# One 512-column matmul for an operand's high and low part in four more projections, and gate logarithms taken straight from the sigmoid

## Chip, cores and metric

The kernel runs on one core of a Trainium2 chip. The metric is the device time of one execution in microseconds (us), the median of the runs shown. The engines are named as the profile names them: PE (TensorE, matmuls), DVE (VectorE), ACT (ScalarE), POOL (GpSimd) and SP (SyncE, which issues DMAs). Each runs its own instructions in order and waits on semaphores for the others.

## The reference, cut to what matters

Two blocks of a network work on one sequence of 256 tokens with 2048 channels, all in float32. The first block:

```python
mod = silu(c) @ w_ada + b_ada                      # sh1, sc1, g1, sh2, sc2, g2
z = (x * (1 + sc1) + sh1) @ w_in + b_in            # 2048 -> 9216: u, v, z_h, z_g
y_a = (gelu(u) * spatial_mix(layer_norm(gelu(v)))) @ w_branch_a
y_b = hyena(short_conv(z_h)) @ w_branch_b          # long convolutions by FFT
mix = (sigmoid(g_a) * y_a + sigmoid(g_b) * y_b) @ w_o + b_o
x = layer_norm(ALPHA * x + g1 * mix)
f = square(relu((x * (1 + sc2) + sh2) @ w_m1 + b_m1)) @ w_m2 + b_m2
x = layer_norm(ALPHA * x + g2 * f)
```

The second block has two layers. The first is a gated convolution: `h @ conv_w_in` (2048 to 6144), a depthwise convolution of 31 taps, a norm, a gate, `@ conv_w_out`. The second is a linear attention with 16 heads of 128 channels, in two directions:

```python
q, a_f, a_b, i, z = split(rms_norm(x) @ hgrn_w_in)           # 2048 -> 10240
log_f = logaddexp(log(lb), log1p(-lb) + log_sigmoid(a))      # = log(lb + (1 - lb) * sigmoid(a))
key = (1 - lb) * sigmoid(-a)
# with b = cumsum(log_f): scores[t, s] = sum over channels of q_t * key_s * exp(b_t - b_s)
o = rms_norm(o_fwd + o_bwd) * o_norm
x = x + (o * silu(z)) @ hgrn_w_out
```

## The kernel before

Activations lie with channels on the 128 partitions and the 256 tokens along a row. To keep float32 accuracy with PE's faster fp32r format, every operand is split into a high part (rounded to fp32r) and a low part (the rest). A product is the sum of three: high weights times high operand, high weights times low operand, low weights times high operand.

Weights stream once through the kernel, in "halves": a half is 8 tiles of 128x128 (512 KB) and holds one half of the input channels of one output block of 128 channels. SP loads halves in the order of the list `HALVES` into a ring of 4, later 6 slots; for each, ACT writes the high part `wh` (L1640, `hi(h)`) and DVE the low part `wl` (L942, `lo(h)`), four buffers each, three halves ahead of PE. An output block of a projection of 2048 channels is two halves, 16 tiles k. Between the halves, in the first block up to the middle of `w_o` and in the first half of the MLP, SP also loads "chunks" of `w_ada`, 512 KB each, and DVE adds one a block (L961, `add_chunk`).

PE accumulates an output block in one of three PSUM banks (`ps[0]` to `ps[2]`). The list `MAIN` says which semaphore tells that a bank is free, and PE's `bank()` waits for the use three before. A bank has 512 columns, and a block 256.

Two forms of the inner loop exist. `half` does three matmuls of 256 columns for each k (L528, L529, L530) into 256 columns of the bank. `wide_half`, in the MLP alone, sends the operand's high and low part through PE as one matmul of 512 columns (L541), and the low weights with the high part as one of 256 (L543) into the first half of the bank. Whoever empties a wide bank adds its two halves: in the MLP ACT reads columns 256:512 (with bias or scale) and DVE adds columns 0:256 (L1338, L1357).

In the input projection (`N_IN`, 72 blocks, the first 24 of them for the hyena branch) ACT empties the bank in one instruction: Identity with the bias for blocks 0 to 23 (L1757), after which DVE does the short convolution (L1084, L1086, L1088), Gelu for 24 to 39 (L1759), Sigmoid for 40 to 71 (L1761). The FFT work of `hyena()` and the spatial gating of `spatial()` are woven in between the blocks as generators. Squares for the variance of the spatial gating are taken by ACT (L1722) and summed by PE (L581).

In the heads (`HG_PARTS`, 5 parts of 2 halves for each of 16 heads, 10 halves a head) the order of the head's own work is written out by `HEAD_PLAN`: head hd makes its step s behind half 10*hd + 6 + s ("tick"), on every engine, for 22 steps. So a head begins at tick 6 of its ten, while two older ones are still under way. Its steps on each engine:

- After part 4 (tick 5) DVE scales the gates (L1577, L1581), ACT takes two sigmoids and a third for z (L2059, L2061, L2065). DVE then computes lb + (1 - lb) * sigmoid (L1591) and its maximum with 2^-64 (L1593), and the keys (L1598).
- Step 0: ACT takes Ln of both gates (L2006). Step 1: DVE sums them up (L1534).
- Steps 1 to 14, nine levels: DVE differences (L1517), ACT exponentials (L2022), POOL products (L2231, L2233), PE scores (L879) into one of three banks, and DVE's predicated copy (L1527) that empties it. PE's next score into a bank waits for the copy of the level three before.
- Steps 16 to 21: PE multiplies with the values (L888), ACT squares (L2027), PE sums (L581), ACT takes Sqrt (L2035), DVE the reciprocal (L1545) and two products (L1548, L1552), ACT and POOL split the result (L2040, L2083).

ACT works with function tables; an ACT_TABLE_LOAD row stands ahead of a function whose table isn't loaded. In the last projection three output blocks (`NEARLY`) start early, between the last head's steps, and ask for all three banks at once.

Of the kernel before, what the change touches and what calls it, by code (L numbers as in the profile page):

```python
# [18 lines left out]
ALPHA = 2.0 ** 0.25  # L19
# [128 lines left out]
HEAD_STEPS = 22  # L148
# [17 lines left out]
def n_rest(k):  # L166
# [21 lines left out]
    "hmade_v hmade_a zin zh uv gate "  # L188
# [3 lines left out]
    "ablo gy mx woe gp "  # L192

    "lg rel rad rsq m2e res "
# [3 lines left out]
    "lbd lbt hg sm sp szs f2 f3 kk0 kk1 zz qq vi "  # L198
    "ln0 ln1 cum0 cum1 dif0 dif1 exp0 exp1 kq0 kq1 sco0 sco1 pla0 pla1 plv0 plv1 vtr vcp "
    "om osq ocp oss osd orc on"  # L200
# [35 lines left out]
def _build(nc, ctx, d, out):  # L236
# [76 lines left out]
    gate = lambda i: BF[:, 40 + i, :] if i < 24 else XR[:, i - 16, :]  # L313
    pad = [misc[:, 2048 + 260 * i:2048 + 260 * i + 258] for i in range(2)]
# [29 lines left out]
    lbtab = misc[:, 512:640]  # L344
    one_row = misc[:, 768:1024]
# [46 lines left out]
    for n in range(16):  # L392
        MAIN.append((s.woe, n + 1))
        if n == 8:
            MAIN.append((s.mod, 10))
# [25 lines left out]
    def wait_placed(w, hd, li):  # L421
        u = hd % 2
        if li == 0:
            w.wait_ge((s.pla0, s.pla1)[u], hd // 2 + 1)
        else:
            w.wait_ge((s.plv0, s.plv1)[u], 8 * (hd // 2) + li)

# [84 lines left out]
    def tensor_program(e):  # L512
# [20 lines left out]


        def wide_half(h, pb, both, ready, first, last):
            hi, lo = wh[h % NSPLIT], wl[h % NSPLIT]
            w.wait_ge(s.lo, h + 1)
            for k in range(8):
                ready(k)
                xs = both(k)  # L540
                e.matmul(pb.rearrange("p (a t) -> p a t", a=2), hi[:, k, :], xs, start=first and k == 0,  # L541
                         stop=False)
                done = e.matmul(pb[:, 0:256], lo[:, k, :], xs[:, 0, :], start=False, stop=last and k == 7)  # L543
            done.then_inc(s.mm, 1)


        def two_halves(h, first, second, ready, begin, end, behind=lambda k: None):
            for j in range(2):
                w.wait_ge(s.lo, h + j + 1)
            for k in range(8):  # L550
                ready(k)
                for j, (pb, xs) in enumerate(((first, A2), (second, A2))):
                    hi, lo = wh[(h + j) % NSPLIT], wl[(h + j) % NSPLIT]
                    x = xs[:, :, 8 * (not begin) + k, :]
                    if pb.shape[1] == 512:
                        e.matmul(pb.rearrange("p (a t) -> p a t", a=2), hi[:, k, :], x, start=begin and k == 0, stop=False)
                    else:
                        e.matmul(pb, hi[:, k, :], x[:, 0, :], start=begin and k == 0, stop=False)
                        e.matmul(pb, hi[:, k, :], x[:, 1, :], start=False, stop=False)
                    done = e.matmul(pb[:, 0:256], lo[:, k, :], x[:, 0, :], start=False, stop=end and k == 7)  # L560
# [13 lines left out]
        def a_tiles(part):  # L574
            return lambda k: (Ah[:, 8 * part + k, :], Al[:, 8 * part + k, :])

        def b_tiles(base):
            return lambda k: (Bh[:, base + k, :], Bl[:, base + k, :])
# [117 lines left out]
        for i, n in enumerate(N_IN):  # L696
            pb = bank()[:, 0:256]
            for part in range(2):
                half(2 * i + part, pb, a_tiles(part), lambda k: wait_lo(w, 8 * part + k, 0),
                     part == 0, part == 1)  # L700
                if part == 0:
                    if 33 <= i < 41:
                        w.wait_ge(s.uv, i - 24)
                        w.wait_ge(s.spec, 16)
                        row_sum(ps[3][:, 0:256], 1, vv(i - 33), i - 33, 8, s.vmean)
# [53 lines left out]
        for n in range(16):  # L759
            pb = bank()[:, 0:256]  # L760
# [12 lines left out]
        for fh in range(2):  # L773
# [4 lines left out]
            for n in range(2, 32):  # L778
                pb = bank()[:]
                for part in range(2):  # L780
                    wide_half(H_M1[fh] + 2 * n + part, pb, lambda k: A2[:, :, 8 * part + k, :],
# [1542 lines left out]
```

## Time and profile before

| | |
|---|---|
| median of 3 runs | 2782.59 us (2781.21 to 2788.07) |
| the profiled execution | 2780.93 us, its span 2779.1 us |
| mean granted TensorE clock | 0.967 |
| PE busy | 2582.7 us, 93% of the span |
| weight loads on PE busy | 2430.1 us, 87% |
| DVE busy | 2018.7 us, 73% |
| ACT busy | 1401.7 us, 50% |
| POOL busy | 840.3 us, 30% |
| DMA | 534.84 MB, mean 192 GB/s |

A row of the timeline has the start, the duration, the engine, the line, the operation, what it writes and reads, how many such instructions follow each other, and in brackets how long the engine was idle before and what ended the wait. Two matmuls overlap, so the distance of their starts, not their duration, tells the pace. Stages by time: filters and `w_ada` to 137, input projection to 655, the two branches' projection to 757, `w_o` to 856, MLP to 1613, convolution input to 1966, convolution output to 2096, heads to 2657, last projection to the end.

### The profile page before, as it was taken

The page shows a single profiled execution, that of the slowest core. Times are in us where ns is not written, and L with a number is a line of the kernel's source. Part 1 is how long each engine was busy: PE and PEld are TensorE (multiplying, and loading weights), DVE is VectorE, ACT ScalarE, POOL GpSimd, SP SyncE. Part 2 cuts the span into 40 slices and gives each one's busy share as a digit, 9 for nine tenths or more (in the row PEclk, how much of TensorE's full clock was granted, in tenths as well). Part 3 has the DMA queues.
Part 4 walks back from the last instruction along what each step waited for, and adds up shares of the span by engine and source line. Part 5 has one row for each costly group of instructions (what it writes and reads, how often), then busy time and mean ns, then how long its engine had stood idle before and what let it go on. Part 6 is the DMA issues. An engine that isn't in the chain of part 4 may idle for free.

```text
span 2779.1 us, 46348 instructions
## 1 busy us (share of the span) xinstructions
PE 2582.7 (93%) x18408; PEld 2430.1 (87%) x18408; DVE 2018.7 (73%) x2576; ACT 1401.7 (50%) x2108; POOL 840.3 (30%) x780
## 2 busy tenths in 40 slices
PE   4599998999997999999999979997799999999989
PEld 1489998999996888888888879987699999999979
DVE  7888765767867876555555568887657899999964
ACT  0154323344435543444544456666556777777753
POOL 0100000001214621001101058888102666666630
PEclk9799999999998999999999989999899999999989
DMA  9978754787873877665566535554355444444434
GB/s 320 340 257 268 231 200 156 239 267 242 270 246 116 291 258 227 190 189 183 190 194 189 185 101 167 167 159 128 102 171 158 150 152 152 150 147 149 148 105 146
DMA packets 146353, 534.84 MB, mean 192 GB/s; under 512 B 16631, under 2 KB 16792, under 8 KB 145688
## 3 DMA queue, kind: packets, MB, share of 16 engines
q1 hardware_dynamic: 143176, 520.33, 58.2%
q0 software_dynamic: 2960, 11.54, 1.2%
q8 instruction: 146, 2.39, 0.3%
q14 instruction: 71, 0.58, 0.1%
HBM read 525.51 MB, written 6.29 MB: 191 GB/s over the span
## 4 chain that ended last, share of the span: by engine, by line
PE 58%; DVE 16%; issue 7%; POOL 7%; ACT 6%; DMA 5%; SPq 0%; POOLq 0%; DVEq 0%; ACTq 0%
PE ps L541 13%; PE ps L528 11%; PE ps L530 10%; PE ps L529 10%; PE ps L543 7%; DVE wl L942 5%; POOL misc L2200 5%; DMA ring<-in_w_ada 4%; ACT wh L1640 2%; DVE AF L961 1%; PE ps L581 1%; DVE BF L1527 1%; PE ps L663 1%; PE ps L651 1%; DVE BF L1517 1%
## 5 line engine op out<-in xcount | busy, mean ns | idle before, releaser
L942 DVE TENSOR_TENSOR wl<-ring,wh 128x1024 fp32r<-128x1024 f32 x784 | 1031.4, 1328 | 381.7 <-ACT wh L1640 380.8
L528 PE MATMUL ps<-A,wh 128*128 128x256 f32 x3424 | 997.2, 291 | 17.0 <-DVE wl L942 10.4
L1640 ACT CAST wh<-ring 128x1024 fp32r<-128x1024 f32 x784 | 814.8, 1043 | 381.5 <-PE ps L530 212.2
L529 PE MATMUL ps<-A,wh 128*128 128x256 f32 x3424 | 974.4, 285 | 0.0
L530 PE MATMUL ps<-A,wl 128*128 128x256 f32 x3424 | 974.3, 285 | 0.0
L528 PEld LDWEIGHTS ps<-A,wh 128*128 128x128 f32 x3424 | 663.1, 194 | 21.8 <-issue 10.8
L529 PEld LDWEIGHTS ps<-A,wh 128*128 128x128 f32 x3424 | 663.3, 194 | 1.2
L530 PEld LDWEIGHTS ps<-A,wl 128*128 128x128 f32 x3424 | 662.2, 193 | 0.0
L541 PE MATMUL ps<-B,wh 128*128 128x512 f32 x1024 | 357.9, 394 | 0.0
L541 PE MATMUL ps<-A,wh 128*128 128x512 f32 x960 | 337.5, 396 | 2.2 <-DVE wl L942 2.2
L543 PE MATMUL ps<-B,wl 128*128 128x256 f32 x1024 | 287.3, 281 | 0.0
L543 PE MATMUL ps<-A,wl 128*128 128x256 f32 x960 | 269.5, 281 | 0.0
L528 PE MATMUL ps<-B,wh 128*128 128x256 f32 x768 | 228.9, 298 | 21.3 <-DVE B L946 7.3
L2200 POOL TENSOR_TENSOR misc<-misc 128x256 f32<-128x256 f32 x224 | 226.7, 1012 | 55.8 <-ACT misc L1915 28.3
L2083 POOL TENSOR_TENSOR B<-tmpA,B 128x256 fp32r<-128x256 f32 x80 | 80.2, 1002 | 524.7 <-ACT B L1867 447.5
L541 PEld LDWEIGHTS ps<-B,wh 128*128 128x128 f32 x1024 | 192.9, 188 | 42.8
L529 PE MATMUL ps<-B,wh 128*128 128x256 f32 x768 | 222.6, 290 | 0.0
L530 PE MATMUL ps<-B,wl 128*128 128x256 f32 x768 | 222.5, 290 | 0.0
L541 PEld LDWEIGHTS ps<-A,wh 128*128 128x128 f32 x960 | 181.2, 189 | 44.6 <-DVE wl L942 2.8
L543 PEld LDWEIGHTS ps<-B,wl 128*128 128x128 f32 x1024 | 194.6, 190 | 0.0
L2231 POOL TENSOR_TENSOR BF<-BF 128x256 f32<-128x256 f32 x128 | 152.5, 1191 | 137.9 <-ACT BF L2022 104.8
L543 PEld LDWEIGHTS ps<-A,wl 128*128 128x128 f32 x960 | 182.4, 190 | 0.0
(247 smaller groups left out, 3323.3 us busy)
## 6 DMA issues: line engine op xcount, KB each, us to landing
ring<-in_w_m SPq DMA_DIRECT2D x256, 512.0 KB, 4.5
ring<-in_hgrn_w_in SPq DMA_DIRECT2D x160, 512.0 KB, 3.8
ring<-in_w_ada SPq DMA_DIRECT2D x144, 512.0 KB, 6.6
ring<-in_w_in SPq DMA_DIRECT2D x144, 512.0 KB, 4.9
ring<-in_conv_w_in SPq DMA_DIRECT2D x96, 512.0 KB, 3.9
AF<-in_w_ada SPq DMA_DIRECT2D x48, 512.0 KB, 9.1
ring<-in_w_ab SPq DMA_DIRECT2D x32, 512.0 KB, 5.2
ring<-in_w_o SPq DMA_DIRECT2D x32, 512.0 KB, 5.4
```

The lines of the kernel that those rows point to most:

```text
L528: e.matmul(dst, hi[:, k, :], xh, start=first and k == 0, stop=False)
L529: e.matmul(dst, hi[:, k, :], xl, start=False, stop=False)
L530: done = e.matmul(dst, lo[:, k, :], xh, start=False, stop=last and k == 7)
L541: e.matmul(pb.rearrange("p (a t) -> p a t", a=2), hi[:, k, :], xs, start=first and k == 0, stop=False)
L543: done = e.matmul(pb[:, 0:256], lo[:, k, :], xs[:, 0, :], start=False, stop=last and k == 7)
L581: e.matmul(bank_ap, ones[:, row, :], tile, start=i == 0, stop=i == n - 1).then_inc(signal, 1)
L651: done = e.matmul(ps[5 + ri][:, mm * 256:mm * 256 + 256], dft[:, 2 * ri + tt, mm * P:mm * P + P], ut[:, tt, :], start=tt == 0, stop=tt == 1)
L942: e.tensor_tensor(low[:], ring[SLOT[h]][:], hi[:].bitcast(F32), ALU.subtract).then_inc(s.lo, 1)
L1640: e.copy(wh[h % NSPLIT][:], ring[SLOT[h]][:]).then_inc(s.hi, 1)
L2083: e.tensor_tensor(low, src, hi.bitcast(F32), ALU.subtract).then_inc(signal, 1)
L2200: padd.up(e.tensor_tensor(pa, pa, ptmp[padd.n % NTMP], ALU.add))
L2231: e.tensor_tensor(sides(BF, at(u, 10 + x), h, h), sides(BF, at(u, 1), h, 256 + h), sides(BF, ev, h, 256 + h), ALU.mult).then_inc(kq, 1)
```

## The change

Four more projections use the wide form: the input projection, `w_o`, the convolution's output and the last one. `half` and `wide_half` become one, with the choice by the width of the target:

```diff
+        def k_tile(dst, hi, lo, x, first, last):
+            if dst.shape[1] == 512:
+                e.matmul(dst.rearrange("p (a t) -> p a t", a=2), hi, x, start=first, stop=False)
+            else:
+                e.matmul(dst, hi, x[:, 0, :], start=first, stop=False)
+                e.matmul(dst, hi, x[:, 1, :], start=False, stop=False)
+            return e.matmul(dst[:, 0:256], lo, x[:, 0, :], start=False, stop=last)
...
-                xh, xl = tiles(k)
-                e.matmul(dst, hi[:, k, :], xh, start=first and k == 0, stop=False)
-                e.matmul(dst, hi[:, k, :], xl, start=False, stop=False)
-                done = e.matmul(dst, lo[:, k, :], xh, start=False, stop=last and k == 7)
+                done = k_tile(dst, hi[:, k, :], lo[:, k, :], tiles(k), first and k == 0, last and k == 7)
```

Input projection: ACT writes columns 256:512 plus the bias, DVE adds columns 0:256, and Gelu or Sigmoid is applied one block later, in place. A bank is now free after DVE's addition (`MAIN`), and the mean of v is summed by PE one block later.

```diff
-        MAIN.append((s.zin, i + 1) if i < 24 else (s.uv, i - 23) if i < 40 else (s.gate, i - 39))
+        MAIN.append((s.zin, i + 1) if i < 24 else (s.pre, i - 23))
...
+        def add_halves(i, dst, pb):
+            w.wait_ge(s.ev, i + 1)
+            return e.tensor_tensor(dst, dst, pb[:, 0:256], ALU.add)
...
             if i < 24:
+                add_halves(i, pad[i % 2][:, 1:257], pb).then_inc(s.zin, 1)
                 short_conv(i, pad[i % 2], zh(i))
+            else:
+                add_halves(i, in_tile(n), pb).then_inc(s.pre, 1)
...
+        def nonlinear(i):
+            x = in_tile(N_IN[i])
+            w.wait_ge(s.pre, i - 23)
+            if i < 40:
+                e.activation(x, x, ACT.Gelu).then_inc(s.uv, 1)
+            else:
+                e.activation(x, x, ACT.Sigmoid).then_inc(s.gate, 1)
...
-                e.activation(pad[i % 2][:, 1:257], pb, ACT.Identity, bias=col("b_in", n)).then_inc(s.zin, 1)
-            elif i < 40:
-                e.activation(uu(n) if n < 8 else vv(n - 8), pb, ACT.Gelu, bias=col("b_in", n)).then_inc(s.uv, 1)
+                e.activation(pad[i % 2][:, 1:257], pb, ACT.Identity, bias=col("b_in", n)).then_inc(s.ev, 1)
             else:
-                e.activation(gate(n - ZG), pb, ACT.Sigmoid, bias=col("b_in", n)).then_inc(s.gate, 1)
+                e.activation(in_tile(n), pb, ACT.Identity, bias=col("b_in", n)).then_inc(s.ev, 1)
+            if i >= 25:
+                nonlinear(i - 1)
```

`w_o` (and the second MLP projection, where it stood already) on DVE, and the two residual projections:

```diff
+        def both_halves(n, alpha, evicted, pb, factor):
+            w.wait_ge(s.ev, evicted)
+            own.up(e.scalar_tensor_tensor(XR[:, n, :], XR[:, n, :], alpha, tmpA[n % 4][:], ALU.mult, ALU.add))
+            w.wait_ge(s.own, own.n)
+            e.scalar_tensor_tensor(XR[:, n, :], pb[:, 0:256], factor, XR[:, n, :], ALU.mult, ALU.add).then_inc(s.xr, 1)
...
+        def add_out(n, pb):
+            own.up(e.tensor_tensor(XR[:, n, :], XR[:, n, :], pb[:, 256:512], ALU.add))
+            w.wait_ge(s.own, own.n)
+            e.tensor_tensor(XR[:, n, :], XR[:, n, :], pb[:, 0:256], ALU.add).then_inc(s.xr, 1)
```

Heads: DVE's L1591 and L1593 go; ACT's Ln reads the sigmoid with (1 - lb) as its scale and lb as its bias, and lb is raised to at least 2^-64 once in the table. The deviation becomes Ln and Exp of -0.5 on ACT, and DVE's reciprocal goes. All of this comes one step later (24 steps instead of 22), and ACT takes the heads of a tick in another order: a head at step 0 first, then one beyond step 15, then the rest.

```diff
-                    w.wait_ge(s.sp, hd + 1)
+                    w.wait_ge(s.sm, hd + 1)
                     w.wait_ge(s.lbt, 4)
...
-                        own.up(e.tensor_scalar(x, x, om, lb, ALU.mult, ALU.add))
-                        w.wait_ge(s.own, own.n)
-                        e.tensor_scalar(slot(u, 6 + k), x, 2.0 ** -64, None, ALU.max).then_inc((s.f2, s.f3)[u], 1)
...
+            for k in range(2):
+                e.activation(slot(u, 6 + k), sig[0][:, 256 * k:256 * k + 256], ACT.Ln,
+                             scale=lbtab[:, 32 * k + 16 + hd:32 * k + 17 + hd],
+                             bias=lbtab[:, 32 * k + hd:32 * k + hd + 1]).then_inc((s.ln0, s.ln1)[u], 1)
...
-            e.activation(ost[u], mean_ap, ACT.Sqrt, scale=1.0 / 128, bias=sm[:, 1:2]).then_inc(s.osd, 1)
+            e.activation(ost[u], mean_ap, ACT.Ln, scale=1.0 / 128, bias=sm[:, 1:2]).then_inc(s.ols, 1)
+            w.wait_ge(s.ols, hd + 1)
+            e.activation(ost[u], ost[u], ACT.Exp, scale=-0.5).then_inc(s.osd, 1)
...
-            e.reciprocal(ost[u], ost[u]).then_inc(s.orc, 1)
-            w.wait_ge(s.orc, hd + 1)
...
-            for hd, _ in HEAD_PLAN[tick]:
+            for hd, step in sorted(HEAD_PLAN[tick], key=lambda x: 0 if x[1] == 0 else 1 if x[1] > 15 else 2):
```

The branches' projection, the convolution's input and the heads' input keep three matmuls of 256 columns.

## Rows read from the trace of the kernel before

**Rows 1.** Windows: PE, PEld, DVE, ACT, POOL busy (x); clock, DMA share, GB/s.

```profile
165.70:240.50 74.80, 74.80 (x626) 74.80 (x625) 64.50 (x80) 32.03 (x39) 0.00 (x0) 1.00 0.84 278
...
2189.20:2651.90 462.70, 448.67 (x3745) 445.69 (x3744) 431.50 (x533) 337.30 (x533) 281.11 (x247) 1.00 0.49 149
```

**Rows 2.** What ended PE's idle time before L879 (us, times).

```profile
  DVE BF L1527: 15.1, 14
```

**Rows 3.** Timeline of ACT, input projection, first and last of 14 evictions.

```profile
165.68 0.48 ACT L1757 ACTIVATE misc<-ps,vec 128x256 f32<-128x256 f32 x1 [1.78 <-PE ps L530]
...
240.56 0.48 ACT L1757 ACTIVATE misc<-ps,vec 128x256 f32<-128x256 f32 x1 [1.77 <-PE ps L530]
```

**Rows 4.** Timeline of DVE, MLP projection without chunks, first and last of nine.

```profile
1302.33 0.42 DVE L1338 TENSOR_TENSOR tmpA<-ps,tmpA 128x256 f32<-128x256 f32 x1 [0.88 <-ACT tmpA L1865]
...
1346.71 0.42 DVE L1338 TENSOR_TENSOR tmpA<-ps,tmpA 128x256 f32<-128x256 f32 x1 [0.88 <-ACT tmpA L1865]
```

**Rows 5.** Timeline of DVE, one block of the input projection.

```profile
206.51 0.41 DVE L1084 TENSOR_SCALAR BF<-misc,vec 128x256 f32<-128x256 f32 x1 [0.84 <-ACT misc L1757]
...
208.17 1.28 DVE L961 SCALAR_TENSOR_TENSOR XR<-ring,cnd,XR 128x1024 f32<-128x1024 f32 x1 [0.20 <-DMA ring<-in_w_ada]
...
209.37 2.35 DVE L942 TENSOR_TENSOR wl<-ring,wh 128x1024 fp32r<-128x1024 f32 x2
```

**Rows 6.** DMA issues in 930:1070: count, KB, median us to landing.

```profile
ring<-in_w_ada SPq DMA_DIRECT2D x24, 512.0 KB, 6.8
```

**Rows 7.** Timeline of DVE, MLP projection with chunks, first and last of eleven.

```profile
919.37 0.41 DVE L1338 TENSOR_TENSOR tmpA<-ps,tmpA 128x256 f32<-128x256 f32 x1
...
974.31 0.42 DVE L1338 TENSOR_TENSOR tmpA<-ps,tmpA 128x256 f32<-128x256 f32 x1 [0.28 <-ACT tmpA L1865]
```

**Rows 8.** Timeline of ACT, around the first gate blocks.

```profile
427.59 1.28 ACT L1761 ACT_TABLE_LOAD   x1
...
447.34 0.47 ACT L1761 ACTIVATE BF<-ps,vec 128x256 f32<-128x256 f32 x1 [4.27 <-PE ps L530]
```

**Rows 9.** Timeline of PE, the second sum of squares.

```profile
451.60 2.39 PE L581 MATMUL ps<-misc,ones 128*128 128x256 f32 x8 [0.99 <-ACT misc L1722]
```

**Rows 10.** Timeline of DVE, `w_o`, the first residual.

```profile
771.30 0.43 DVE L1225 SCALAR_TENSOR_TENSOR XR<-XR,tmpA 128x256 f32<-128x256 f32 x1 [9.11 <-DMA XR<-in_x]
```

**Rows 11.** Timeline of PE, behind `w_o`.

```profile
864.64 1.22 PE L751 MATMUL ps<-misc,ones 128*128 128x256 f32 x2 [8.17 <-POOL misc L2139]
```

**Rows 12.** Timeline of PE, heads: before and at the wait, behind part 4.

```profile
2224.58 0.28 PE L528 MATMUL ps<-A,wh 128*128 128x256 f32 x1
...
2226.18 0.68 PE L879 MATMUL ps<-BF 128*128 128x128 f32 x4 [1.08 <-DVE BF L1527]
...
2250.58 0.50 PE L879 MATMUL ps<-BF 128*128 128x128 f32 x3
```

**Rows 13.** Timeline of DVE, the same head and the next.

```profile
2222.95 1.75 DVE L1545 RECIPROCAL misc<-misc 128x256 f32<-128x256 f32 x1
...
2225.59 0.43 DVE L1527 COPY_PREDICATED BF<-masks,ps 128x256 f32<-128x256 uint8 x1
...
2254.66 0.41 DVE L1591 TENSOR_SCALAR misc<-misc 128x256 f32<-128x256 f32 x1 [2.21 <-ACT misc L2061]
...
2256.89 0.61 DVE L1598 TENSOR_SCALAR BF<-misc 128x256 f32<-128x256 f32 x2
```

**Rows 14.** Timeline of ACT, table loads of a head.

```profile
2248.16 1.28 ACT L2035 ACT_TABLE_LOAD   x1
...
2252.03 1.28 ACT L2059 ACT_TABLE_LOAD   x1
...
2255.89 1.28 ACT L2006 ACT_TABLE_LOAD   x1
```

**Rows 15.** Timeline of PE, behind the last head's last half.

```profile
2662.82 0.55 PE L528 MATMUL ps<-B,wh 128*128 128x256 f32 x1 [5.36 <-issue]
```

**Rows 16.** Timeline of DVE, the last head's values.

```profile
2662.20 0.41 DVE L1606 TENSOR_TENSOR misc<-ps,statb 128x256 f32<-128x256 f32 x1
```

More of the change, by code:

```diff
@@ L553, in two_halves @@
                     hi, lo = wh[(h + j) % NSPLIT], wl[(h + j) % NSPLIT]
[L554 to L560, printed above, removed]
+                    done = k_tile(pb, hi[:, k, :], lo[:, k, :], xs[:, :, 8 * (not begin) + k, :], begin and k == 0,
+                                  end and k == 7)
                     if k == 7:
@@ L780, in tensor_program @@
                 for part in range(2):
-                    wide_half(H_M1[fh] + 2 * n + part, pb, lambda k: A2[:, :, 8 * part + k, :],
+                    half(H_M1[fh] + 2 * n + part, pb, a_tiles(part),
                               lambda k: wait_lo(w, 8 * part + k, 1), part == 0, part == 1)
@@ L838, in next_square @@
             row_sum(mean_ap, 2, lsq[0][:, n % 2 * T:n % 2 * T + T], n, 16, s.sqs)
+        conv_tile = lambda k: Bl.rearrange("p (a k) t -> p a k t", a=2)[:, :, k, :]
         for n in range(16):
-            pb = bank()[:, 0:256]
+            pb = bank()[:]
             for part in range(2):
-                half(H_CO + 2 * n + part, pb, lambda k: (Bl[:, 8 * part + k, :], Bl[:, 16 + 8 * part + k, :]),
+                half(H_CO + 2 * n + part, pb, lambda k: conv_tile(8 * part + k),
                      lambda k: wait_lo(w, 8 * part + k, 3), part == 0, part == 1)
@@ L915, in tensor_program @@
                     heads_behind(x)
-        early = [bank()[:, 0:256] for n in range(NEARLY)]
+        early = [bank()[:] for n in range(NEARLY)]
         done_heads = lambda k: w.wait_ge(s.blo, 85 + k + 1)
@@ L1288, in vector_program @@
             w.wait_ge(s.khat, 144)
-            residual(n, ALPHA if n < 12 else 1.0, s.woe, n + 1)
+            both_halves(n, ALPHA if n < 12 else 1.0, EV_O + n + 1, pb, mod[:, 32 + n:33 + n])
             if n < 8:
@@ L1541, in head @@
                 yield
-            for _ in range(4):
+            for _ in range(5):
                 yield
             w.wait_ge(s.osd, hd + 1)
-            e.reciprocal(ost[u], ost[u]).then_inc(s.orc, 1)
-            w.wait_ge(s.orc, hd + 1)
             w.wait_ge(s.ocp, hd + 1)
@@ L1825, in scalar_program @@
             e.activation(tmpA[n % 4][:], pb, ACT.Identity, scale=mod[:, 32 + n:33 + n],
[L1826 removed]
+                         bias=gb[:, n:n + 1]).then_inc(s.ev, 1)
             squares_early(n, 0)
@@ L1864, in scalar_program @@
                 w.wait_ge(s.blo, 21 + 32 * fh + n - 3)
-                e.activation(tmpA[n % 4][:], pb, ACT.Identity, bias=col("b_m1", 32 * fh + n)).then_inc(s.rel, 1)
+                e.activation(tmpA[n % 4][:], pb, ACT.Identity, bias=col("b_m1", 32 * fh + n)).then_inc(s.ev, 1)
                 w.wait_ge(s.rsq, 32 * fh + n + 1)
@@ L1876, in scalar_program @@
                 if fh:
-                    e.activation(tmpA[n % 4][:], pb, ACT.Identity, scale=mod[:, 80 + n:81 + n]).then_inc(s.m2e, 1)
+                    e.activation(tmpA[n % 4][:], pb, ACT.Identity, scale=mod[:, 80 + n:81 + n]).then_inc(s.ev, 1)
                     squares_early(n, 1)
@@ L2235, in head @@
                 yield
-            for _ in range(5):
+            for _ in range(6):
                 yield
```

96 lines of the change are left out of this document (39 added, 57 removed).

## Prediction

> **What bounds the kernel now.** I read the page's first part (the table above), then the windows, then the timelines of single engines stage by stage. TensorE (PE) fills 100% of the input projection (165.7:240.5) and 97% of the heads (2189.2:2651.9), where DVE is at 93%, both at a granted clock of 1.00, the 2.4 GHz level [rows 1]. So two things can be won: PE time itself, and the few waits in which PE stands still. The biggest repeated one is L879 (a head's scores) behind L1527 (a predicated copy on DVE): 15.1 us in 14 times [rows 2].
>
> **Term 1, the matmuls.** In the projections that change, one weight tile k costs three matmuls of 256 columns; afterwards one of 512 and one of 256. Before, ACT's evictions L1757 go from 165.68 to 240.56 in 13 periods: 5.760 us for the 16 tiles of one output block [rows 3]. The wide form already runs in the MLP: DVE's L1338 goes from 1302.33 to 1346.71 in 8 periods, 5.547 us for 16 tiles [rows 4]. The difference is 0.213 us a block (13.3 ns a tile). I take it whole wherever PE sets the pace.
>
> Here the Trainium skill speaks against the size. "TensorE: Matmul & The Clock Gate", Back-to-back issue gap, puts the warm gap of isolated matmuls at N/2.4 + 2.5 ns, so one matmul less would give 2.5 ns a tile and not 13.3; for 1920 tiles 4.8 us against 25.6. The rows of this kernel show 13.3 with the same operands, each matmul with its weight load, and I go by them.
>
> *Input projection, 72 blocks.* Block 0 waits for its operand, so it gains nothing: 71 x 0.213 = 15.1. What the halves' addition adds: one DVE operation a block. Its price is that of L1338, which also adds a PSUM half, 0.42, with the wait between dependent operations 0.45. DVE's round from L1084 at 206.51 to the end of the pair at 211.72 is 5.21, of it 0.20 a wait for a DMA [rows 5]: 5.01 + 0.45 = 5.46, under 5.547, with 0.09 to spare. The chunk of w_ada is the next thing that can be late: its median to landing is 6.8 us in the MLP's first half, which loads the same two halves and one chunk a block [rows 6], and there L1338 goes from 919.37 to 974.31 in 10 periods, 5.49 [rows 7]. So the DMA queue has carried this pace. I charge 0.7 us for 24 blocks; the ends are 0 and 5.1 (no gain in them at all). From block 24 on ACT writes Identity, DVE adds, and ACT applies Gelu or Sigmoid a block later: 0.47 more a block on an ACT that is 43% busy [rows 1, 8] and hidden by the three halves of weights that lie ready. One spot isn't: the first Sigmoid's table load, 1.28, stands at 427.59 in ACT's idle time now. Afterwards it comes behind the eviction of block 41 (447.34), ahead of the weight cast that DVE and then the squares wait for; PE waits for these squares at 451.60 [rows 8, 9]. Charge: 1.28 + 0.47, rounded to 1.7; ends 0 and 1.8. Sum of the stage: 15.1 - 0.7 - 1.7 = 12.7.
>
> *w_o, 16 blocks.* DVE stands until x has landed by DMA at 771.3 [rows 10], PE runs dry behind it, and the weight low part it needs lies behind L1225 in DVE's queue. Blocks 0 and 1 gain nothing (the landing doesn't move), and the second operation of `both_halves` (0.45, as above) makes the restart later. At the end PE waits 8.17 us for POOL's chain of sums L2139 [rows 11], which starts with the squares of block 14, so block 15 gains nothing. 13 x 0.213 - 0.45 = 2.3.
>
> *Convolution output, 16 blocks.* Block 0 waits for its operand. The second addition lies inside each block's slack, but not behind the last: 15 x 0.213 - 0.45 = 2.7.
>
> *Last projection, 16 blocks.* 13 ordinary ones, 2.8; of the three early ones (0.6), which run between the steps of the last head, I take 0.3; the last addition ahead of the output costs 0.45: 2.6.
>
> Term 1 together: 12.7 + 2.3 + 2.7 + 2.6 = 20.3 us.
>
> **Term 2, the heads.** At 2224.58 PE starts a weight tile; the next group would start 0.36 later and starts at 2226.18, 1.24 late, and takes 0.07 longer: 1.31 us [rows 12]. DVE is what is late: it spends 1.75 on the reciprocal L1545 and 0.9 on two products, and L1527 ends at 2226.02. Ahead of that it waits 2.21 for the second sigmoid and does L1591 and L1593 twice, 2.2 us (2254.66 to 2256.89 in the next head) [rows 13]. The change takes both away: the gate's affine part goes into ACT's scale and bias, the floor 2^-64 into the table, the reciprocal into Ln and Exp of -0.5. DVE drops 1.75 + 2.2 = 3.95 us of 33 a head (431.5 over 13 heads).
>
> ACT's order changes too. Now a head has five table loads of 1.28, four of them for Sqrt, Exp, Sigmoid and Ln between 2248.16 and 2257.17 [rows 14]. The sorting puts the gates' Ln, then the deviation's Ln and Exp of an older head, in one tick: Sigmoid, Ln, Exp, three loads. That saves 2.56 and adds about 0.47 (Exp) and 0.3 (two Ln for one).
>
> The Trainium skill, "ScalarE: Activation LUTs", Table sets: the hidden batching unit, says that one set holds both ln and exp. This kernel's rows show a load between its Ln and its Exp all the same, so I count three loads; by the page it would be two, and the margin below 1.28 wider.
>
> What is late next: counted from PE's L879 behind part 4 (2250.58, [rows 12]), with durations as they stand, L1577 ends by about 1.6, the three sigmoids by 3.3, ACT's weight cast by 4.3; DVE's low part 5.5 and the copy that stalled PE 5.9, needed at 9.9, three halves of 3.3 on. ACT goes on: Ln's load 5.6, three Ln 6.9, Exp's load 8.2, Exp 8.65, the next cast 9.65; then DVE's low part 10.85, the head's two products 11.75, the next copy 12.1. PE needs that copy at 13.3 and those weights at 13.7. So the wait goes, with 1.2 us to spare. POOL (281 of 463 us busy) isn't near. Of the 14 waits 13 are worth 1.31. Behind the last head PE stands 5.36 us until 2662.82 because all three banks are asked for and the third is free only after L1606, which ends at 2662.61 [rows 15, 16]; that DVE work comes only 0.3 earlier while PE comes 1.3 earlier. 13 x 1.31 + 0.3 = 17.3. Ends: 5 (the margin is missed by a microsecond in each head) and 22 (the wait for the banks halves as well). The tail of the last head trades a Sqrt and the reciprocal (1.75) for Ln, a load (1.28) and Exp: nothing.
>
> **Sum.** 20.3 + 17.3 = 37.6. The profiled execution took 2780.93 (span 2779.1 and 1.8 around it), so 2743.3. The median of the runs shown is 1.7 above it: 2745.
>
> **Rivals.** (a) The chain of ACT in the heads is longer than 8.65, and part of the wait stays: DVE now waits for Exp where it computed the reciprocal itself. For it: 1.2 us of margin in a chain of twelve steps; against it: ACT has lost two loads. Up to 12 us less: 2748 to 2757. (b) DVE and the chunks bind in the input projection: 0.09 us of spare on DVE is thin. Up to 5 us less: 2750. (c) The wait for the banks behind the last head, and the low clock after it, shrink with DVE's load: 3 to 6 us more, 2739 to 2742. (d) The wide pair is no cheaper in the changed stages than three matmuls: the 112 blocks lose 0.213 each, 2745 + 24 = 2769; only another behaviour of PE than in [rows 4] could do it. The Trainium skill's gap (above) would leave 2.5 of the 13.3 ns: by it 2765. (e) The other side: ACT's burst between Sigmoid and the next weight cast becomes PE's wait. PE has 3 us until the weights of that tick (10.85 against 13.7); to reach the time before, the burst must eat these 2.9, the 1.31, and 20.3 / 14 = 1.45 more, so it decides from 5.7 us beyond my chain, over four table loads a head more than I count. That would be 2783 and above.
>
> **How the numbers follow.** Forecast 0.55, (a) 0.20, (b) 0.09, (c) 0.08, (d) 0.03, (e) 0.05. The forecast's own range is 2741 to 2750. The range that leaves out 2 in 10 at most is 2737 to 2760: (c) below, (a) above. A measurement of this kernel tells about 0.3%, 8.3 us, from no change. Faster by more than that means under 2774: 0.91; within it 0.05 ((a) and (d) together, part of (e)); slower 0.04.
>
> **What would show it.** A profile after should have blocks of 5.55 us in evictions of the input projection and in the last projection, a period of a head of 34.3 for now 35.6, no idle time of L879 behind L1527, three table loads a head, DVE at some 85% in the heads, and a longer wait at 451.60. I am wrong if the head's period stays above 35, if L528's place shows waits for weight low parts L942 in the first 24 blocks, or if ACT loads a table between the gates' Ln and the deviation's Ln.

## The result: 15 us faster where 38 were forecast

| | before | after |
|---|---|---|
| median, both in the same set of runs | 2786.95 us (5 runs) | 2772.03 us (2767.39 to 2772.26, 5 runs) |
| once more, in another set (below) | 2786.39 us (11 runs) | 2769.71 us (2763.65 to 2776.41, 6 runs) |
| profiled execution | 2780.93 us | 2772.07 us, span 2770.3 us |
| PE busy | 2582.7 us | 2567.9 us |
| DVE busy | 2018.7 us | 2016.2 us |
| ACT busy | 1401.7 us | 1393.4 us |

The ratio is 0.9947, 95% interval 0.9934 to 0.996, so 14.9 us; the second set gives 0.9944 (0.9922 to 0.9965), 16.7 us. The forecast, 2745 us and 2737 to 2760, is missed by 27 us: 22.7 are missing gain (14.9 where 37.6 were forecast), and 4.4 come from where it started, a median before of 2782.59 us from three runs where five give 2786.95. The two profiled executions differ by 8.9 us only, and they differ in more than the change (the pace of wide tiles and the late chunks, below). So the profiles show mechanisms, and the medians what the change is worth.

The windows that answer to [rows 1]: input projection, and the heads up to 2640.

```profile
165.70:240.50 74.80, 74.25 (x429) 64.63 (x427) 71.89 (x98) 33.39 (x41) 0.00 (x0) 1.00 0.85 286
2189.20:2640.00 450.80, 441.34 (x3688) 438.36 (x3687) 388.13 (x466) 305.36 (x524) 272.54 (x245) 1.00 0.46 151
```

PE still stands still in the heads (441 of 451 us), while DVE's share has fallen from 93% to 86%.

ACT's evictions in the input projection, first and last of 14, which answer to [rows 3]:

```profile
165.11 0.48 ACT L1759 ACTIVATE misc<-ps,vec 128x256 f32<-128x256 f32 x1 [1.67 <-PE ps L535]
...
237.22 0.48 ACT L1759 ACTIVATE misc<-ps,vec 128x256 f32<-128x256 f32 x1 [1.66 <-PE ps L535]
```

13 periods of 5.547 us, the same as those of [rows 4]: the wide pair does give 0.213 us a block in the new place too. The same unchanged loop of the MLP that gave 5.547 before is slower now, DVE's first and last of nine:

```profile
1299.80 0.42 DVE L1344 TENSOR_TENSOR tmpA<-ps,tmpA 128x256 f32<-128x256 f32 x1 [0.97 <-ACT tmpA L1868]
...
1345.03 0.42 DVE L1344 TENSOR_TENSOR tmpA<-ps,tmpA 128x256 f32<-128x256 f32 x1 [0.98 <-ACT tmpA L1868]
```

45.23 / 8 = 5.654 us, at a granted clock of 1.00. Between 1260 and 1550 us this costs 5 us.

In the heads, waits from 2220 to 2560 us (total, times, longest), which answer to [rows 2]:

```profile
DVE wl L938 <- ACT wh L1634: 46.1, 19, 3.5
...
PE ps L858 <- ACT misc L2040: 7.8, 10, 0.8
...
DVE BF L1595 <- ACT misc L2073: 3.3, 9, 0.4
```

The wait of the scores for DVE's copy is gone, as forecast. In its place PE waits for ACT's copy of the older head's output (L2040) before it transposes the values (L858):

```profile
2241.69 0.41 PE L858 MATMUL ps<-ident,misc 128*128 128x128 f32 x2 [0.79 <-ACT misc L2040]
```

The row to look at is the first of the three, though: DVE now waits 46 us for ACT's weight casts. DVE's timeline shows a head's period (its sums L1540) and the two waits in it; ACT's shows what stands ahead of the second cast, which answers to [rows 14], and where ACT itself waits for DVE.

```profile
2225.74 1.76 DVE L1540 TENSOR_TENSOR_SCAN misc<-misc,BF 128x256 f32<-128x256 f32 x2
...
2253.22 1.62 DVE L938 TENSOR_TENSOR wl<-ring,wh 128x1024 fp32r<-128x1024 f32 x1 [1.29 <-ACT wh L1634]
...
2258.65 1.22 DVE L938 TENSOR_TENSOR wl<-ring,wh 128x1024 fp32r<-128x1024 f32 x1 [3.44 <-ACT wh L1634]
...
2260.98 1.77 DVE L1540 TENSOR_TENSOR_SCAN misc<-misc,BF 128x256 f32<-128x256 f32 x2
```

```profile
2250.65 0.63 ACT L2073 ACTIVATE misc<-misc 128x512 f32<-128x512 f32 x1 [0.67 <-DVE misc L1584]
...
2252.15 1.03 ACT L1634 CAST wh<-ring 128x1024 fp32r<-128x1024 f32 x1
2253.20 1.28 ACT L2014 ACT_TABLE_LOAD   x1
2254.50 1.09 ACT L2014 ACTIVATE BF<-misc 128x256 f32<-128x256 f32 x2
2255.50 0.45 ACT L2046 ACTIVATE misc<-ps,sm 128x256 f32<-128x256 f32 x1
2255.97 1.28 ACT L2048 ACT_TABLE_LOAD   x1
2257.26 0.42 ACT L2048 ACTIVATE misc<-misc 128x256 f32<-128x256 f32 x1
2257.59 1.98 ACT L1634 CAST wh<-ring 128x1024 fp32r<-128x1024 f32 x2
```

A head takes 35.27 us (mean of ten), for 35.61 before and 34.3 forecast. DVE idles 5.1 us in it: 0.37, 1.29 and 3.44. So its own work is 30.2. Before, DVE idled 2.2 us a head, all in one place ([rows 13]), and its own work was 33.4. In both kernels the period is DVE's own work plus DVE's waits for ACT: 33.4 + 2.2 = 35.6 and 30.2 + 5.1 = 35.3. Such a sum alone proves nothing, since work and idle time make up the period on every engine. What it adds is whom DVE waits for: never for PE or POOL, only for instructions of ACT, and ACT's chain in front of them starts with a wait for DVE's L1584. So the two can form a closed round that keeps its length whatever PE does. Call this **DVE's round** (theory A). The competing reading (theory B) is the forecast's: PE has a period of its own, 34.3, and loses what it waits at one spot.

For the projections the profile shows late chunks. PE's sums over w_ada, one in the input projection, one in `w_o`, one in the MLP:

```profile
241.14 1.58 PE L566 MATMUL ps<-ones,XR 128*128 128x1 f32 x13 [1.18 <-DVE XR L957]
...
802.59 2.07 PE L566 MATMUL ps<-ones,misc 128*128 128x1 f32 x14 [0.79 <-DVE misc L957]
...
973.37 1.84 PE L566 MATMUL ps<-ones,misc 128*128 128x1 f32 x8 [4.75 <-DVE misc L957]
```

Behind the first two, windows of the same kernel (before, both stretches were at 1.00):

```profile
244.00:246.00 2.00, 2.00 (x8) 1.72 (x7) 0.40 (x1) 0.00 (x0) 0.00 (x0) 0.50 0.67 236
...
805.00:810.00 5.00, 5.00 (x17) 4.23 (x17) 1.31 (x2) 0.00 (x0) 0.00 (x0) 0.50 0.62 202
```

The clock stands at 0.50, the 1.2 GHz level. The wide tiles' starts, counted against 0.347 us a tile, give its cost: 1.6 us at 244, 2.7 at 805 and 2.2 at 977 (the expectation of experiment 6 puts the three at 1.5, 2.3 and 1.7).

### The profile page after: what moved, and what is told of

Its sections match the earlier page's. It is cut to its first block, busy times and chain, and to the rows that moved or that the text cites. A ratio compares the mean times of both kernels' runs of the same rounds, so it can differ in the third digit from the quotient of the medians.

```text
span 2770.3 us, 42622 instructions
## 1 busy us (share of the span) xinstructions
PE 2567.9 (93%) x16488; PEld 2321.7 (84%) x16488; DVE 2016.2 (73%) x2617; ACT 1393.4 (50%) x2161; POOL 814.7 (29%) x780
## 4 chain that ended last, share of the span: by engine, by line
PE 64%; DVE 12%; POOL 7%; issue 6%; ACT 6%; DMA 5%; SPq 0%; POOLq 0%; DVEq 0%; ACTq 0%
PE ps L531 29%; PE ps L535 19%; POOL misc L2214 5%; PE ps L533 4%; PE ps L534 4%; DVE wl L938 4%; DMA ring<-in_w_ada 3%; ACT wh L1634 2%; PE ps L576 2%; DVE AF L957 2%; PE ps L875 1%; PE ps L658 1%; PE ps L566 1%; POOL misc L2153 1%; PE ps L646 1%
## 5 line engine op out<-in xcount | busy, mean ns | idle before, releaser
L938 DVE TENSOR_TENSOR wl<-ring,wh 128x1024 fp32r<-128x1024 f32 x784 | 1036.7, 1335 | 398.9 <-ACT wh L1634 357.6
L531 PE MATMUL ps<-A,wh 128*128 128x512 f32 x2176 | 780.7, 403 | 19.1 <-DVE A L942 9.0
L533 PE MATMUL ps<-A,wh 128*128 128x256 f32 x2304 | 677.3, 294 | 15.7 <-DVE A L942 10.6
L531 PE MATMUL ps<-B,wh 128*128 128x512 f32 x1792 | 645.6, 404 | 22.9 <-DVE B L942 7.3
L534 PE MATMUL ps<-A,wh 128*128 128x256 f32 x2304 | 657.2, 285 | 0.0
L531 PEld LDWEIGHTS ps<-A,wh 128*128 128x128 f32 x2176 | 414.2, 190 | 121.0 <-issue 14.4
L533 PEld LDWEIGHTS ps<-A,wh 128*128 128x128 f32 x2304 | 447.6, 194 | 20.6 <-issue 11.6
L534 PEld LDWEIGHTS ps<-A,wh 128*128 128x128 f32 x2304 | 447.7, 194 | 1.2
L531 PEld LDWEIGHTS ps<-B,wh 128*128 128x128 f32 x1792 | 342.6, 191 | 108.0 <-issue 11.7
L535 PEld LDWEIGHTS ps<-B,wl 128*128 128x128 f32 x1792 | 345.4, 193 | 0.5
L2214 POOL TENSOR_TENSOR misc<-misc 128x256 f32<-128x256 f32 x224 | 226.7, 1012 | 55.8 <-ACT misc L1918 28.2
L2245 POOL TENSOR_TENSOR BF<-BF 128x256 f32<-128x256 f32 x128 | 154.8, 1209 | 110.6 <-ACT BF L2032 68.4
L2247 POOL TENSOR_TENSOR BF<-BF 128x256 f32<-128x256 f32 x128 | 148.1, 1157 | 0.0
L1918 ACT ACTIVATE misc<-misc,vec 128x256 f32<-128x256 f32 x240 | 109.7, 501 | 54.9 <-POOL misc L2214 30.2
L1523 DVE TENSOR_TENSOR BF<-misc 128x512 f32<-128x512 f32 x128 | 121.3, 948 | 4.3 <-POOL BF L2247 3.8
L957 DVE SCALAR_TENSOR_TENSOR XR<-ring,cnd,XR 128x1024 f32<-128x1024 f32 x75 | 96.0, 1280 | 6.0 <-DMA ring<-in_w_ada 5.7
```

The lines of the kernel that those rows point to most:

```text
L531: e.matmul(dst.rearrange("p (a t) -> p a t", a=2), hi, x, start=first, stop=False)
L533: e.matmul(dst, hi, x[:, 0, :], start=first, stop=False)
L534: e.matmul(dst, hi, x[:, 1, :], start=False, stop=False)
L535: return e.matmul(dst[:, 0:256], lo, x[:, 0, :], start=False, stop=last)
L938: e.tensor_tensor(low[:], ring[SLOT[h]][:], hi[:].bitcast(F32), ALU.subtract).then_inc(s.lo, 1)
L957: chunks.up(e.scalar_tensor_tensor(acc, wt, cnd[:, k:k + 1], acc, ALU.mult, ALU.add))
```

## The experiments

All times are medians. The first four kernels ran together (before: 2788.27 us, 17 runs), the next four (before: 2786.39, 11 runs) and the last four (before: 2785.87, 19 runs) too.

**1 and 2. Each half of the change alone.** The first has all edits outside the heads, the second only those in the heads.

> The four projections take the wide form, the heads stay as they were. If the gains of the two parts simply add, this kernel is faster than the one before by what the marks of the two traces give the projections: 8.1 us in the input projection, 2.8 in the convolution's output, 2.7 in the last one, against 1.4 lost in w_o and 3.6 at the late chunk in the MLP; together 8 to 10 us. My forecast had 20.3 us. If the loss lies in something that the two parts do to each other, this kernel alone would show the 20 us.

> Only the heads change, the projections keep three matmuls of 256. Theory A (DVE's round sets the head's period: its own work and its waits for ACT, 33.4 + 2.2 us before, 30.2 + 5.1 after): period 35.3 for 35.6, 4 to 6 us faster in all. Theory B (my forecast: PE's own 34.3 us once the copies aren't late, and the missing rest is an effect of the wide projections around): 17 us faster.

Projections alone: 2773.73 us, ratio 0.9945 (0.9927 to 0.9963), 14.5 us faster, with 10 to 20 in the interval. Heads alone: 2782.25 us, 0.998 (0.9964 to 0.9995), 6.0 us faster, with 1.4 to 10. The head's period is 35.60 in the first and 35.28 in the second. So the heads gave about a third of their 17.3 us with nothing wide around them: theory A's number. The two medians add up to 20.5 us where the whole change has 14.9 and 16.7, which the three intervals allow. The projections gave more than the 8 to 10 us that I had read from one pair of profiles, and the forecast's 20.3 is at the edge of their interval.

**3. ACT's weight cast earlier.** `hi` is what casts a half. The last two lines of the diff are DVE's order in the tick.

```diff
-                    hi(H_HG + x + 3)
+                    if hd < 2 or x % 10 != 7:
+                        hi(H_HG + x + 3)
...
             e.activation(ost[u], mean_ap, ACT.Ln, scale=1.0 / 128, bias=sm[:, 1:2]).then_inc(s.ols, 1)
+            if hd < 14:
+                hi(H_HG + 10 * hd + 30)
             w.wait_ge(s.ols, hd + 1)
...
-            for hd, _ in HEAD_PLAN[tick]:
+            for hd, step in sorted(HEAD_PLAN[tick], key=lambda x: x[1] > 15):
```

> The kernel after, with ACT's weight cast of tick 7 pulled ahead of the second table load (between the two logarithms and the exponential of the deviation), and DVE taking the new head's sums ahead of the old head's two products in that tick. No work is removed. Theory A (DVE's round): DVE's 3.4 us wait for that cast shrinks to about 1.5, its round to some 33.4, so the head's period falls from 35.3 to PE's own 34.2 to 34.4 and the kernel gains 11 to 14 us on the one after. Theory B (PE's wait for the copy of the last head's output on ACT sets the period by itself): that copy's place on ACT isn't touched, so the period stays at 35.3 and the time too.

2757.59 us, ratio 0.9892 (0.9872 to 0.9912): 30.7 us under the kernel before, where the kernel after is 14.9 and 16.7 under it; so 14 to 16 us of gain, where theory A said 11 to 14. From the first to the last head's sums the trace is 15.2 us shorter than the one after. DVE's timeline has both waits shorter, and the next head 34.30 us on:

```profile
2228.59 1.27 DVE L1540 TENSOR_TENSOR_SCAN misc<-misc,BF 128x256 f32<-128x256 f32 x2
...
2257.71 1.23 DVE L938 TENSOR_TENSOR wl<-ring,wh 128x1024 fp32r<-128x1024 f32 x1 [0.72 <-ACT wh L1634]
...
2261.41 1.23 DVE L938 TENSOR_TENSOR wl<-ring,wh 128x1024 fp32r<-128x1024 f32 x1 [2.11 <-ACT wh L1634]
...
2262.89 1.26 DVE L1540 TENSOR_TENSOR_SCAN misc<-misc,BF 128x256 f32<-128x256 f32 x2
```

Its window of the heads:

```profile
2189.20:2640.00 450.80, 450.80 (x3789) 450.08 (x3788) 395.51 (x472) 319.31 (x540) 285.97 (x248) 1.00 0.47 154
```

PE is busy all the time, L2040's place on ACT was not touched, and PE's wait for it is gone. DVE now waits for PE too, 0.5 us in each head before L1584, which it never did in the kernel after. The period is the 34.3 of the forecast: now PE sets it.

**4. The transposition a step later.** PE's `step` first, then that of ACT's copy of the values.

```diff
-                if step == 6:
+                if step == 7:
...
-                if step == 7:
+                if step == 8:
```

> The kernel after, with PE's transposition of the values (and ACT's copy of them) one step later, so that the new wait of PE for ACT's copy of the older head's output is gone. Theory A (DVE's round): PE's wait goes elsewhere, behind a copy or a weight low part of DVE, the period stays 35.2 to 35.3 and the time within 2 us of the kernel after. Theory B (this wait sets the period): 34.2 to 34.4, 13 us faster than the one after.

2770.08 us, ratio 0.9935 (0.9916 to 0.9954): 18.2 us under the kernel before, so 1.5 to 3.3 us beyond the kernel after, which is within the noise. The wait for L2040 is gone and the period is unchanged, 35.26 us:

```profile
2255.17 1.76 DVE L1540 TENSOR_TENSOR_SCAN misc<-misc,BF 128x256 f32<-128x256 f32 x2
2290.44 1.76 DVE L1540 TENSOR_TENSOR_SCAN misc<-misc,BF 128x256 f32<-128x256 f32 x2
```

So the wait at which PE stood was not what cost the time. Removed, half of it comes back in other places (0.4 us of 0.8 in each head, behind L1533 and L938 of DVE), and DVE's three waits are what they were. Theory B falls.

**5. The kernel after once more.**

> The kernel after once more, unchanged, beside the kernels of this call. The pace of a wide weight tile (a matmul of 512 and one of 256) took one of two values in all profiles so far, 347 or 353 ns, for stretches of 30 to 300 us. If that is a matter of the execution, the profiled execution has its 353 ns stretches at other places than the first one had (1260 to 1540 us), and the execution's time moves by 6.6 ns for each tile in them; if it is a matter of the program, they are at the same places.

2769.71 us. The profile (2776.41 us) has the slow pace from 240 to 300, 880 to 980, 1260 to 1550 and 2700 us to the end; the first one had it from 760 to 800, 980 to 1070 and 1260 to 1550. Those are the longer stretches; one program, two patterns, with the longest stretch in common.

**6. The sums later.** PE's `reduce_chunks` and DVE's `bias` of blocks 16, 32, 48 and 64 of the input projection, of block 8 of `w_o` and block 16 of the MLP move from behind the block's first half to behind its second:

```diff
-                    if i in n_ada:
-                        reduce_chunks(n_ada[i])
...
+            if i in n_ada:
+                reduce_chunks(n_ada[i])
```

> The kernel after, with PE's sums over w_ada's chunks (and DVE's bias behind them) moved half an output block back in the input projection, w_o and the first MLP projection. No work changes. In the profile after, PE waits there 1.3, 0.9 and 0.8 us in the input projection, 0.9 in w_o and 4.9 in the MLP, and behind three of these five waits (at 244, 805 and 977 us) its clock falls to the 1.2 GHz level, which costs 1.5, 2.3 and 1.7 us. Theory C (a late chunk makes PE wait, and the wait brings the low clock): the first four waits are gone and about 2 us of the fifth are left, the low clock at 244 and 805 is gone too: 9 to 11 us faster than the one after. Theory D (the low clock comes with the stage, whatever PE waits for): only the waits go, 6 to 7 us faster, and the low stretches stay.

2755.4 us, ratio 0.9891 (0.9871 to 0.9911), 14.3 us under the kernel of experiment 5, more than either theory gave (9 to 11, and 6 to 7); the two intervals leave some 8 us either way. PE's sums in its timeline have no wait any more:

```profile
240.91 1.92 PE L566 MATMUL ps<-ones,XR 128*128 128x1 f32 x16
...
798.19 1.84 PE L566 MATMUL ps<-ones,misc 128*128 128x1 f32 x16
...
962.39 1.84 PE L566 MATMUL ps<-ones,misc 128*128 128x1 f32 x16
```

Its windows at the two places, and that of experiment 8 (which has the same sums) at the first:

```profile
244.00:246.00 2.00, 2.00 (x13) 1.72 (x13) 1.94 (x5) 0.14 (x1) 0.00 (x0) 1.00 0.62 184
...
800.00:810.00 10.00, 10.00 (x58) 8.79 (x58) 5.03 (x7) 3.60 (x4) 0.00 (x0) 1.00 0.54 184
```

```profile
246.00:248.00 2.00, 2.00 (x8) 1.71 (x7) 1.96 (x5) 0.00 (x0) 0.00 (x0) 0.50 0.74 190
```

Four of the five waits I named were sums. The fifth, at 498 (0.65 us idle), is PE waiting for DVE's L1111 of the hyena branch; it was my misreading, and it stays. The low clock at 805 and 977 goes with the waits, as theory C says. That at 244 is not so simple: it is gone here, and experiment 8 has it at 246 without a wait (some 1.5 us).

All 14 profiles together show how far theory C holds. The sums over `w_ada`, without the last one, come seven times in each. PE waits over 0.6 us ahead of 44 of them, and the low clock is at 37 of these; it is at 2 of the other 54. The longest wait that left the clock at 1.00 is 1.43 us, at 242.8 in experiment 7. So the low clock nearly always needs the wait, but doesn't always follow it, and what else decides stays open.

**7. `w_o` alone back to three matmuls.** On PE and ACT the bank is 256 columns again, and DVE keeps one operation:

```diff
-            pb = bank()[:]
+            pb = bank()[:, 0:256]
...
-            both_halves(n, ALPHA if n < 12 else 1.0, EV_O + n + 1, pb, mod[:, 32 + n:33 + n])
+            w.wait_ge(s.ev, EV_O + n + 1)
+            e.scalar_tensor_tensor(XR[:, n, :], XR[:, n, :], ALPHA if n < 12 else 1.0, tmpA[n % 4][:], ALU.mult,
+                                   ALU.add).then_inc(s.xr, 1)
```

> The kernel after, with w_o alone back at three matmuls of 256, ACT's eviction of the whole sum and one operation on DVE. From PE's restart behind the branches' projection to the first matmul of the MLP the one before took 121.6 us and the one after 123.1, where my forecast had 119.3. Theory E (the wide form costs w_o more than it gives, through a late chunk at its ninth block and the low clock behind the two waits): the stretch takes 121.6 again and the kernel is 1 to 2 us faster than the one after. Theory F (the wide form does give 2.8 us there, and something carried over from the stage before costs 4): the stretch takes 124 to 126.

2767.01 us, ratio 0.9935 (0.9916 to 0.9954). The stretch took 122.8 us, between the two theories (all these numbers run on to the last matmul of the MLP's first two blocks, 20.6 us behind the first one, in every kernel alike); the wide form takes 123.1 and 121.7 in its two profiles, and 119.0 and 119.8 with the later sums (experiments 6 and 8). The narrow `w_o` also waits 1.6 us for its chunk and then runs at the low clock. So neither theory holds as it stands. It isn't the wide form that makes the chunk late, as E had it, and the stretch isn't as long as F had it. The gain of 2.7 us on experiment 5 is within the noise. With the wait out of the way the wide form is at the forecast's 119.3.

**8. Experiments 3 and 6 together.**

> The third kernel's order in the heads and the sixth's later sums together, on the kernel after. If the two mechanisms are separate, their gains add: 12 to 14 us from the heads (period 34.3) and 6 to 11 from the sums, so 18 to 25 us faster than the kernel after.

2740.45 us, ratio 0.9841 (0.982 to 0.9863), 29.3 us under the kernel of experiment 5; the sums alone gave 14.3, the earlier cast (30.7 - 14.9 or 16.7) 14 to 16. They add, and the total is above the 18 to 25 that I expected because both parts were.

**9. Only ACT's part of experiment 3.**

> Of the third kernel's two edits only ACT's: the weight cast of tick 7 ahead of the second table load. DVE keeps the old head's products ahead of the new head's sums, so they wait for the exponential, which now ends 1.0 us later (about 9.7 us behind PE's scores instead of 8.7), where the products began at 10.8 before. By theory A DVE's round loses 1.1 us and is then as long as PE's own: period 34.2 to 34.4, 13 us faster than the kernel after. If the order on DVE was what helped in the third kernel, the period stays above 35.

2757.65 us, ratio 0.9896 (0.987 to 0.9922), 28.2 us under the kernel before and so 11.5 to 13.3 under the one after; period 34.30. The cast alone does it. Only the second head's period, 33.9 in experiment 3, is 35.4 here.

**10. A reciprocal more on DVE**, into a new tile:

```diff
                 elif part == 0:
+                    e.reciprocal(spare[:], rstd)
```

> The kernel after with one instruction more for each head on DVE, a reciprocal of 256 columns whose result nobody reads, in the tick behind a head's first output block, where DVE doesn't wait for anybody. By theory A (DVE's round is the period) each head gets longer by all of it, 1.75 us: period 37.0, and the whole kernel 26 to 28 us slower than the one after. If a wait between two engines at one spot set the period, as theory B and my forecast had it, work put elsewhere on DVE would be taken from its slack: period 35.3 to 36.

2792.94 us, ratio 1.0026 (1.0011 to 1.0041): 7.1 us above the kernel before, so 22 to 24 above the kernel after (26 to 28 expected). The added instruction and two sums:

```profile
2253.74 1.76 DVE L1541 TENSOR_TENSOR_SCAN misc<-misc,BF 128x256 f32<-128x256 f32 x2
...
2256.14 1.75 DVE L1599 RECIPROCAL spare<-statb 128x256 f32<-128x256 f32 x1
...
2290.60 1.76 DVE L1541 TENSOR_TENSOR_SCAN misc<-misc,BF 128x256 f32<-128x256 f32 x2
```

The period is 36.86: of the 1.75 us of DVE work, put where nobody waited, 1.59 arrive in every head. From the first to the last head's sums the trace takes 22.1 us more. That is what a period set by DVE's round looks like, and it rules out slack on DVE. DVE's three waits are as long as without it (0.37, 1.29, 3.45); the missing 0.16 us are in DVE's own work. PE waits 2.1 us a head where it waited 0.8.

Experiments 3, 4, 9 and 10 all start from the kernel after. That DVE's round set the period of the kernel before too is read from its trace and not tested.

**11. The last sum too.** DVE's `bias(11)` moves with it.

```diff
-            if fh == 0:
-                reduce_chunks(11)
...
+                    if fh == 0 and n == 0 and q == 1:
+                        reduce_chunks(11)
```

> The eighth kernel (both fixes) with the last of the sums over w_ada moved too: from the end of the first MLP projection to behind the second quarter of the next block. In all profiles PE waits there 3.0 to 4.1 us for the last chunk, and its clock is at the 1.2 GHz level behind it, which costs 1.0 to 2.3 us. If the wait makes the low clock, both go: 4 to 6 us faster than the eighth kernel. If only the wait goes: 3 to 4 us.

2731.99 us, ratio 0.9797 (0.9782 to 0.9812): 8.5 us under experiment 8, more than either expectation; the two were measured in different sets, and their profiled executions, 2739.09 and 2733.36 us, differ by 5.7. First the sum's wait and the window there in experiment 8, then the window of this kernel:

```profile
1056.91 2.54 PE L566 MATMUL ps<-ones,misc 128*128 128x1 f32 x16 [3.32 <-DVE misc L956]
```

```profile
1060.00:1065.00 5.00, 5.00 (x18) 4.28 (x17) 1.00 (x1) 0.13 (x1) 0.00 (x0) 0.52 0.55 172
```

```profile
1055.00:1060.00 5.00, 5.00 (x31) 4.42 (x30) 2.45 (x4) 1.05 (x1) 0.00 (x0) 1.00 1.02 397
```

Here wait and low clock go together: all 13 profiles with this sum in its old place have both. This is the fastest kernel: 54 us under the one before, 37 to 39 under the one after.

**12. The kernel before once more.**

> The kernel before once more. Its first profile had the 353 ns pace in the MLP from 880 to 980 us alone. If the pace belongs to the execution and not to the change, this profile may have it elsewhere or for longer (in the MLP from 1260 to 1540 us, as five of the changed kernels), and the part of the MLP there is then 5.3 us longer, as it was in the profile after.

2785.45 us, ratio 0.9998 (0.9987 to 1.0008). The profiled execution took 2794.1 us, 13.2 more than the first. DVE's rows in the MLP, first and last of nine:

```profile
1301.04 0.43 DVE L1338 TENSOR_TENSOR tmpA<-ps,tmpA 128x256 f32<-128x256 f32 x1 [0.96 <-ACT tmpA L1865]
...
1346.27 0.42 DVE L1338 TENSOR_TENSOR tmpA<-ps,tmpA 128x256 f32<-128x256 f32 x1 [0.97 <-ACT tmpA L1865]
```

5.654 us, here from 980 to 1540 us, which cost 8.8 us. So the slow pace isn't of the change. Nor are the late chunks of the change alone: the four sums that wait in the profile after (7.5 us idle in all) waited 2.2 us in the first profile of before, 7.0 in this one and 5.4 in experiment 2, which has the old projections too; with the wide input projection and the sums in their old place it was 4.7 to 8.3 in seven profiles.

## Why the prediction was wrong, point by point

**What bounds the kernel** was read right for PE, and wrong for the heads. DVE's 93% against PE's 97% looked like an engine with 7% to spare. These 7% were one wait of 2.2 us for ACT inside DVE's own round; it had no other idle time.

**The step that failed** is the price in Term 2, "Of the 14 waits 13 are worth 1.31", which makes 13 x 1.31 of "So the wait goes". The wait did go, and the period fell by 0.34 us a head (35.61 to 35.27) and not by 1.31. The chain that led to it was right: the copy was counted to end 12.1 us behind PE's scores, and it ended 12.1 behind them (2261.1 against 2249.0). The three table loads are there. What the sum took for granted is that a wait that goes gives PE's time back. But DVE lost 3.95 us of its own work by the forecast (3.2 in the trace, since among others the sums take 1.76 where they took 1.48), and its waits for ACT grew from 2.2 to 5.1: my own list has DVE's copy end at 5.9 and the cast that it needs next at 9.65, and I never added such gaps up. With the 29.5 us of work that I left DVE they make about 35, not 34.3. With the cast moved ahead of the table load (experiments 3 and 9) the period is 34.30, and from the first to the last head's sums it is 511.6 us in experiment 3 instead of 532.9: Term 2 was there to be had, and more, for one instruction in another place.

**Term 2** was 17.3 us and measures 6.0: from the first to the last head's sums it was 532.9 us and is 526.8, and the heads alone gave 6.0. The wait for the banks behind the last head was to shrink; it grew from 5.36 to 6.54 (rival (c) falls). Rival (a) named the right neighbourhood, ACT's chain, but had PE keep part of a local wait, and capped it at 12 us of which 11 came. Rival (e)'s burst did make a cast late, 3.44 us for DVE, but PE never waited for those weights itself, and the kernel isn't slower than before.

**Term 1** was 20.3 us and measures 14.5 (10 to 20) alone. In the profile after the convolution's output gives 2.8 (forecast 2.7). The end of the kernel behind the last head's sums is 3.1 us shorter (2.6 and 0.3 forecast). The input projection gives 7.9 of 12.7 from the first to the last eviction: blocks 1 to 15 exactly their 0.213; 2.3 lost at block 16, to the sum's wait and the low clock (I had charged 0.7, for another reason); 0.1 to 0.2 instead of 0.213 in many blocks with other work between them; 2.2 at blocks 41 to 43, with the first Sigmoid's table load (1.7 charged: PE's wait grew by 1.0, and behind it the clock is low from 448.8, where the profile before had 1.00); 0.9 at block 47. `w_o` lost 1.5 where 2.3 was forecast. The chunk waits were the blind spot: PE's sums over the chunks are on its path, and I had looked for late chunks only on DVE, rival (b). How much of them is the change's is only bounded: against the waits in the two profiles of before, between 0.5 and 5.3 us. So is how much of the missing 6 us of Term 1 is the slow pace (7 instead of 13 ns a tile where it rules).

**Rival (d)** is dead: 5.547 in the first blocks. By the Trainium skill, "TensorE: Matmul & The Clock Gate", Back-to-back issue gap, whose gap for isolated matmuls charges 2.5 ns for each, a block would have gained 0.04 us, an estimate from that figure. The trace disagrees: it gained 0.213.

**The signs** I had named: blocks of 5.55, yes; three table loads, yes; DVE at 85%, yes (86); a longer wait at 451.60, yes (2.01 us for 0.99, at 447.56 now); no idle time of L879's place behind the copy, yes but for one wait of 0.9 us; period 34.3, no. The sign of being wrong, a head's period above 35, is what happened. By the Trainium skill, "ScalarE: Activation LUTs", Table sets: the hidden batching unit, one table set holds both Ln and Exp, which would leave two loads. The trace disagrees: a load of 1.28 us stands between them, at 2255.97.

## What to carry to other kernels

In a loop where several engines hand work around, add up each engine's own work and its waits over one period: suspect the engine whose waits are all for a partner that in turn waits for it, even with 14% idle as DVE here; a wait of another engine may only be where the surplus shows. The test is cheap: add work to the suspect where it doesn't wait, and see whether the period takes it. Taking work off such an engine pays only as far as its waits don't grow, and a table load that stands ahead of somebody else's input is such a wait: put the input first. A small dependent step of a full engine (here a sum of 16 tiny matmuls) costs its wait and mostly the low clock behind it; half a block of delay took away the wait in nearly every case.

## What the runs showed of the hardware

A wide tile (512 and 256 columns) takes 347 or 353 ns (blocks of 5.547 or 5.654 us) at the same granted clock of 1.00, for 30 to 560 us at a time. The switches lie where other matmuls or a wait come between the wide ones, at different places in two executions of one program: in the profile after, 800 tiles in a row from 1267.9 us take 353.5 ns each, and behind the next interruption, at 1550, they take 347. Three matmuls of 256 took 360 ns in stages with nothing between them. The wide form is thus worth 13 or 7 ns a tile. The kernel after has 3968 wide tiles where the one before has 2048, so more of its time is open to this. Why one pace or the other is taken wasn't settled.
